# Six 256-column blocks of the second input projection computed in twelve stretches among the mixers' steps

## The reference, cut to what matters

```
a = rms_norm_2(h, norm_attn[i])
u = a @ w_in[i]                                  # 256 x 1024 times 1024 x 3228
(nsa_q, k_cmp, v_cmp, k_slc, v_slc, k_win, v_win, nsa_g,   # 652 columns
 d_q, d_k, d_v,                                  # 3 x 256
 g_q, g_k, g_v, g_lr, g_og,                      # 128, 128, 256, 16, 256
 r_q, r_f, r_i, r_og) = split_cols(u, IN_SPLITS_2)  # 4 x 256
o_a = nsa_attention(...)      # compressed, selected and window attention, gated by sigmoid(nsa_g)
o_b = diff_attention(...)     # two softmax maps per head, subtracted
o_c = gla_mixer(...)          # chunked recurrence, times silu(g_og)
o_d = hgrn2_mixer(...)        # the same recurrence with another gate, times silu(r_og)
h = h + concatenate([o_a, o_b, o_c, o_d]) @ w_out[i]
```

## Time and profile before

| | |
|---|---|
| Runs | 2823.51, 2812.08, 2816.25 us, median 2816.25 |
| Profiled execution | 2825.22 us, of it the span 2823.5 us |
| Busy share | PE 94%, PEld 52%, DVE 22%, ACT 17%, POOL 4% |
| Mean granted clock | 0.922 |

### The profile page before, as it was taken

How to read it: one execution, slowest core, us unless ns; L and a number is a source line. 1 busy time by engine, 2 the same in 40 slices (tenths; PEclk the granted TensorE clock), 3 DMA queues, 4 the chain that set the end, 5 groups by cost and what they waited for, 6 DMA issues and landing times.

```text
span 2823.5 us, 46982 instructions
## 1 busy us (share of the span) xinstructions
PE 2642.1 (94%) x21263; PEld 1474.5 (52%) x21263; DVE 633.8 (22%) x1316; ACT 477.9 (17%) x824; POOL 126.3 (4%) x327
## 2 busy tenths in 40 slices
PE   8899999999989977999999977799999999999997
PEld 7556558666545665444445655444535445353443
DVE  3434523333521432100011432200101000010002
ACT  1421321421222322001012322010000000000001
POOL 4011000011000030000000030000000000000000
PEclk9999999999999756999999756899999999999999
DMA  7321333311334401444434401599999999999990
GB/s 230 115 69 60 119 123 121 130 66 61 120 127 130 133 1 45 134 149 149 143 116 140 131 1 36 211 395 348 368 374 366 385 344 377 369 370 375 355 369 30
DMA packets 181276, 542.26 MB, mean 192 GB/s; under 512 B 26929, under 2 KB 40401, under 8 KB 181073
## 3 DMA queue, kind: packets, MB, share of 16 engines
q1 hardware_dynamic: 167776, 536.95, 52.6%
q10 hardware_dynamic: 12992, 1.22, 0.4%
q0 software_dynamic: 304, 1.05, 0.1%
HBM read 538.12 MB, written 1.05 MB: 191 GB/s over the span
## 4 chain that ended last, share of the span: by engine, by line
PE 89%; ACT 4%; DVE 3%; issue 2%; POOL 1%; DMA 0%; DVEq 0%; SPq 0%; ACTq 0%; POOLq 0%
PE psum L370 27%; PE psum L2310 20%; PE psum L2329 10%; PE psum L529 6%; PE psum L1297 4%; PE psum L2065 3%; PE psum L1958 2%; PE psum L421 1%; PE psum L2285 1%; PE psum L1729 1%; PE psum L2293 1%; PE psum L1708 1%; PE psum L835 1%; PE psum L839 1%; PE psum L2325 1%
## 5 line engine op out<-in xcount | busy, mean ns | idle before, releaser
L370 PE MATMUL psum<-ring,hT 128*128 128x512 f32 (+3 forms) x1856 | 792.5, 586 | 21.6 <-ACT area L642 13.2
L370 PEld LDWEIGHTS psum<-ring,hT 128*128 128x128 f32 x1856 | 355.0, 198 | 417.0 <-issue 384.0
L2310 PE MATMUL psum<-ring,area 128*32 128x448 f32 x4608 | 439.2, 539 | 2.6 <-ACT area L2412 2.0
L2310 PEld LDWEIGHTS psum<-ring,area 128*32 128x32 f32 x4608 | 150.0, 110 | 285.5 <-issue 280.3
L529 PE MATMUL psum<-hT,ring 128*128 128x256 f32 x768 | 170.0, 385 | 0.0
L529 PEld LDWEIGHTS psum<-hT,ring 128*128 128x128 f32 x768 | 148.4, 194 | 21.6 <-issue 1.0
L2329 PE MATMUL psum<-area 128*32 128x256 f32 x2688 | 149.8, 380 | 2.0 <-ACT area L2430 2.0
L2329 PE MATMUL psum<-ring,area 128*32 128x256 f32 x2688 | 151.5, 380 | 0.0
L2310 PE MATMUL psum<-area 128*32 128x448 f32 x1536 | 147.3, 539 | 0.0
L2329 PEld LDWEIGHTS psum<-area 128*32 128x32 f32 x2688 | 85.7, 110 | 60.2 <-ACT area L2430 3.9
L2329 PEld LDWEIGHTS psum<-ring,area 128*32 128x32 f32 x2688 | 84.9, 110 | 57.0 <-issue 2.7
(11 more groups left out here) (491 smaller groups left out, 2462.8 us busy)
## 6 DMA issues: line engine op xcount, KB each, us to landing
ring<-in_w_in_dram SPq DMA_DIRECT2D x92, 1024.0 KB, 5.0
ring<-in_moe_w_gate_dram SPq DMA_DIRECT2D x96, 896.0 KB, 6.8
ring<-in_moe_w_up_dram SPq DMA_DIRECT2D x96, 896.0 KB, 7.7
area<-in_moe_w_down_dram SPq DMA_DIRECT2D x112, 512.0 KB, 7.4
ring<-in_moe_w_down_dram SPq DMA_DIRECT2D x112, 512.0 KB, 6.9
area<-in_moe_w_gate_dram SPq DMA_DIRECT2D x32, 896.0 KB, 6.9
area<-in_moe_w_up_dram SPq DMA_DIRECT2D x32, 896.0 KB, 8.1
ring<-in_w_out_dram SPq DMA_DIRECT2D x16, 1024.0 KB, 5.0
```

Of the source, the lines that this page charges most:

```text
L370: last = nc.tensor.matmul(acc(g)[:, t, 0:d["n"]], lhs(kk, t), w[:, k, :], start=kk == 0, stop=kk == d["nk"] - 1)
L2310: last = nc.tensor.matmul(PS[32 * j:32 * j + 32, 3 * p + b, 0:PIECE], XG[:, k, 32 * b:32 * b + 32], expert_slot(j0 + j // 2, GROUP * (j % ...
```

## The change

The projection's columns are split anew. Four tiles stay in the u stage: 272 columns (g_q, g_k and g_lr), 512 (r_q, r_f), 512 (nsa_q to v_slc) and 396 (k_win, v_win, nsa_g and g_v), 1692 columns. The other 1536 columns are six "fills" of 256 (d_q, d_k, d_v, r_i, g_og, r_og). A fill accumulates both token tiles in one bank, number 2, as 16 matmuls of 256 columns; it yields after every four, and the new plan has its letter f 24 times, always as ff: a stretch is 8 matmuls, half a block, and there are 12. The recurrence gives bank 2 up and goes over two banks, `u % 2`. The norm of d_q and d_k becomes a part of its own (d). The first exponential e stands just after the first g, the two silu gates stand at the end, behind the last fill. The fills' loads stand in LOADS behind those of the compressed attention and ahead of the output projection's. HSB, CS and PCT leave `hT` for the area, as `hT` is read until the last fill.

```diff
-        U_TILES = ((GQ0, GLR0), (GLR0, RQ0), (RQ0, RI0), (NQ0, KW0), (KW0, DK0), (DK0, GQ0), (RI0, COLS2))
+        U_TILES = (((GQ0, GV0), (GLR0, GOG0)), ((RQ0, RI0),), ((NQ0, KW0),), ((KW0, DQ0), (GV0, GLR0)))
+        FILLS = ((DQ0, DK0), (DK0, DV0), (DV0, GQ0), (RI0, ROG0), (GOG0, RQ0), (ROG0, COLS2))
...
+            for piece in FILLS:
+                pieced(("fill", L), A["w_in_2"][L], (piece,), 2)
             pair(("out2", L), A["w_out_2"][L], "dve")
...
         def u_pe(pe, L, fresh):
             gs = group("u", L)
-            for i in range(3):
-                gemm(pe, gs[i], ht_lhs, fresh if i == 0 else None)
-            pe.wait_ge(sem("gemm_out_act"), evacuated(gs[1])[1])
+            gemm(pe, gs[0], ht_lhs, fresh)
+            steps = gemm_steps(pe, [gs[1]], ht_lhs)
+            next(steps)
+            next(steps)
+            pe.wait_ge(sem("gemm_out_act"), evacuated(gs[0])[1])
             transposes(raw((GQ0, P), (GK0, P), (GLR0, 16)), 4).then_inc(sem("m_transposed"), 1)
...
+        def fill_pe(pe, L):
+            for g in group("fill", L):
+                d = TILES[g]
+                gemm_begin(pe, g)
+                landed(pe, d["first"])
+                w = half_view(d["first"], (KD, d["n"]))
+                for t in range(T):
+                    for k in range(KD):
+                        last = nc.tensor.matmul(acc(g)[:, t, :], ht_lhs(k, t), w[:, k, :], start=k == 0, stop=k == KD - 1)
+                        if (t, k) == (T - 1, KD - 1):
+                            last.then_inc(sem("weights_used"), 1)
+                        if k % 4 == 3:
+                            yield
+
+        def fill_act(s, L):
+            for g in group("fill", L):
+                yield
+                yield
+                yield
+                u_out(s, g)
+                yield
...
-        MIXER_PLAN = "cggncvgncgcgtctgacgacegcagcagaaagaeaaagaaagaaagaagaaaggaa"
+        MIXER_PLAN = "cffgencffgcngffcvgffcagcffdcgffdacgacaffadgeaaffgaaagaaffagaaffgaagaagaaffgaagagffv"
...
         def gates_act(s, L):
-            for c in (GOG0, ROG0):
-                s.do(nc.scalar.activation(U2[:, :, c:c + 256], U2[:, :, c:c + 256], ACT.Silu))
             s.after(nc.scalar.activation(GATES.rearrange("p (t g) -> p t g", t=T), U2[:, :, NG0:NG0 + 12], ACT.Sigmoid)
                     .then_inc(sem("m_gates"), 1), "m_gates")
             yield
+            s.do(nc.scalar.activation(U2[:, :, GOG0:GOG0 + 256], U2[:, :, GOG0:GOG0 + 256], ACT.Silu))
+            s.after(nc.scalar.activation(U2[:, :, ROG0:ROG0 + 256], U2[:, :, ROG0:ROG0 + 256], ACT.Silu)
+                    .then_inc(sem("m_gates"), 1), "m_gates")
...
-                if u >= 3:
-                    pe.wait_ge(sem("gla_far"), 16 * L + u - 2)
-                ps = PS[:, u % 3]
+                if u >= 2:
+                    pe.wait_ge(sem("gla_far"), 16 * L + u - 1)
+                ps = PS[:, u % 2]
```

More of the change, by code:

```diff
@@ L253, in pair, with pieced @@
                 TILES.append(dict(group=group, n=512, c0=512 * i, evac=evac, first=first + i, end=first + 3 + i, bank=bank))
-        U_TILES = ((GQ0, GLR0), (GLR0, RQ0), (RQ0, RI0), (NQ0, KW0), (KW0, DK0), (DK0, GQ0), (RI0, COLS2))
+        U_TILES = (((GQ0, GV0), (GLR0, GOG0)), ((RQ0, RI0),), ((NQ0, KW0),), ((KW0, DQ0), (GV0, GLR0)))
+        FILLS = ((DQ0, DK0), (DK0, DV0), (DV0, GQ0), (RI0, ROG0), (GOG0, RQ0), (ROG0, COLS2))
+        def pieced(group, w, pieces, narrow=None):
+            n = sum(b - a for a, b in pieces)
+            per = KD if KD * n <= HALF else KD // 2
+            first = len(LOADS)
+            for k in range(0, KD, per):
+                parts, c = [], 0
+                for a, b in pieces:
+                    parts.append((slice(c, c + b - a), kview(w)[:, k:k + per, a:b]))
+                    c += b - a
+                LOADS.append(((per, n), parts))
+            TILES.append(dict(group=group, n=n, c0=pieces[0][0], pieces=pieces, evac="act", first=first, halves=KD // per,
+                              per=per, nk=KD, end=len(LOADS), narrow=narrow is not None,
+                              bank=2 * (len(TILES) % 2) if narrow is None else narrow))
         CMPW = {}
@@ L1379, in u_pe, with u_out @@
                 .then_inc(sem("gla_z"), 1)
[L1380 to L1383 removed]
+            for _ in steps:
+                pass
+            steps = gemm_steps(pe, [gs[2]], ht_lhs)
+            next(steps)
+            next(steps)
+            pe.wait_ge(sem("gemm_out_act"), evacuated(gs[1])[1])
+            transposes(raw((RQ0, P), (RQ0 + P, P), (RF0, P), (RF0 + P, P)), 6).then_inc(sem("m_transposed"), 1)
+            for _ in steps:
+                pass
+            steps = gemm_steps(pe, [gs[3]], ht_lhs)
+            next(steps)
+            next(steps)
+            pe.wait_ge(sem("gemm_out_act"), evacuated(gs[2])[1])
+            transposes(raw((KC0, P)), 4).then_inc(sem("m_transposed"), 1)
+            for _ in steps:
+                pass
+        def u_out(s, g):
+            d = TILES[g]
+            s.eng.wait_ge(sem("weights_used"), used(d["end"] - 1))
+            c = 0
+            for a, b in d["pieces"]:
+                ins = nc.scalar.activation(U2[:, :, a:b], acc(g)[:, :, c:c + b - a], ACT.Copy)
+                c += b - a
+                if c < d["n"]:
+                    s.do(ins)
+                else:
+                    s.after(ins.then_inc(sem("gemm_out_act"), 1), "gemm_out_act")
         def u_act(s, L):
             gs = group("u", L)
[L1388 to L1395 removed]
+            u_out(s, gs[0])
             s.eng.wait_ge(sem("m_transposed"), 5 * L + 1)
```

152 lines of the change are left out of this document (82 added, 70 removed).

## The result

The changed kernel takes 2794.14 us (median of 4 runs, 2787.21 to 2796.85), the one before on the same chip 2818.46 us (4 runs, 2812.08 to 2823.51): a ratio of 0.991 (95% interval 0.988 to 0.994). It is faster by 24 us, where 57 us were forecast. The time lies in the forecast's wide range, at the weak edge of its mechanism.

What follows compares the result with a forecast made beforehand. PE bounds the u stage; the mixers run at 1.2 GHz with 25.5 us idle. Per layer -41.2 (u stage), +9.5 (mixers), +3 (end): -28.7 us, twice -57: 2768 us profiled, 2758 median; range 2712 to 2818, own range 2738 to 2778.

Steps and rivals of the forecast that it cites:

- The u stage: Second stack's projection stage: three tiles' worth, 48 matmuls of 512 columns, leave; -41.2 us a layer, no new wait.
- The fills: In the mixers: twelve stretches, seven at 3.5 us and five cold at 5.4 us, 52 us a layer; bounds 42.5 to 85.
- The waits: PE's idle time in the mixers: 20 us a layer for 25.5 us; bounds 15 to 35 us.
- The end of the mixers: ACT's copy, table load and two gates behind the last stretch, all on the path: +3 us a layer.
- POOL's wait: PE's 6.7 us wait in the mixers for POOL's factors goes, as the first exponential stands earlier.
- I take it that 5 of 12 start cold: Mixers: five stretches start at the slow clock, a quarter of small work runs slowly; small work 82 us a layer.
- the forecast's scale of 119 to 70 us: PE's work in the mixers other than fills, a layer: 119 us all at slow clock, 70 us all at full clock.
- The first stack: Taken as best analogue for the mixers: small products woven with projection bursts, 40% bursts, mean clock 0.94; fills are 28%.
- Full clock nearly throughout: Rival, mixers: small work 70, fills 42.5, waits 22 us; -48 us a layer, 2720 us; chance 0.18.
- a clock that never rises: Rival, all stretches in the mixers stay slow: 219 us, +36 us a layer, 2889 us; chance 0.06.
- Waits of 35 us: Rival, mixers: ACT's in-order copies make PE wait 35 instead of 20 us a layer; 2788 us; chance 0.14.
- a clock that goes back and forth: Rival, mixers: all twelve stretches start cold, six tenths of small work slow; 182 us, about 2815 us; chance 0.12.

Runs made afterwards that it cites:

- the run with the gates moved: Two silu gates moved ahead of the last attention turn, against the changed kernel with fills respaced and attention exponentials issued early: 2738.33 us, 0.972 of the kernel before.
- fours: Changed kernel with attention exponentials issued early and fills in six stretches of 16 matmuls instead of twelve of 8: 2800.19 us, 0.993 of the kernel before.
- The doubled stretches: Changed kernel with each stretch's 8 matmuls issued twice, the first time without effect: 2854.29 us, 1.015 of the kernel before.
- The second profile of the changed kernel: Changed kernel measured again unaltered, in five rounds: 2792.91 us, 0.991 of the kernel before.
- two banks alone: Kernel before the change with only the recurrence put on two banks instead of three: 2816.78 us, ratio 1.000.
- the first exponential early alone: Kernel before the change with only the plan's first e moved to just behind the first two g: 2804.22 us, ratio 0.995.
- the run with the fills first: Changed kernel with all 24 fill steps at once behind the first compressed step, ahead of the other mixer steps: 2826.53 us, 1.003 of the kernel before.
- the last stretch moved: Changed kernel with the last stretch six steps earlier, right behind the one before it: 2778.75 us, 0.986 of the kernel before.

## Why the prediction was wrong

On the profiled executions the forecast was 2768 us and 2787.2 us came, 19 us more; on the medians the gain was 24 us for 57 us. The difference between the two comparisons is the spread of single executions told above, so the steps are taken from the profiles:

**Right.** The u stage (-41.2 us forecast; -41.2 and -41.2 measured, without a gap). The fills: 52 us forecast, 51.7 and 54.0 measured; 5 and 7 of the 12 stretches took 4.4 us or more, 9 of these 12 less than 5.4 us and one 6.2 us. The waits: 20 us forecast, 20.5 measured. The end of the mixers: +3 forecast, +2.9 measured, and the run with the gates moved shows that it was those 2.5 us of ACT. The two banks: nothing. POOL's wait gone.

**The step that failed: "I take it that 5 of 12 start cold and that a quarter of the small work is done slowly: small work 70 + 0.25 x 49 = 82 us".** Measured were 88.0 and 92.7 us, a share of 0.37 and 0.46; that is 16.7 of the 19 us. The step behind it is the walk through the plan: "The others come after 8 to 14 us". It added up durations at full clock and left out the waits, though the same text counted 20 us of them elsewhere. In the trace six stretches, not four, come after more than 6 us in layer 0 (8.5 to 23.1 us), and the last two after 23.1 and 21.5 us. Both omissions work the same way: the clock falls some 5 us behind a stretch, a wait there uses up some of those fast us, and the rest of the distance runs at the slow clock and is longer still. The last two distances of layer 0 alone hold 28.1 us of small work at the slow clock (15.59 us from 1005 to 1022.85 us, 12.46 us from 1032.3 to 1049.35 us). By the forecast's scale of 119 to 70 us that is an estimated 11.6 us of the 18.0 us above full clock. So the number of cold stretches was nearly right (5 and 7 for 5); what failed is how long the clock stays down before each. The runs show the dependence from both sides: with distances of 16 to 25 us nearly everywhere (fours) the slow share is 0.75 and 0.59, with some 20 short distances 0.14 and 0.08, for the same work.

The first stack is no support for a quarter either, though the mean clock of 0.94 in the earlier trace rows was read rightly: its bursts make up 40%. The doubled stretches make up nearly half of the mixers and still left 0.29 of the small work slow, because the last two distances stayed at 23.1 and 21.5 us. So the share of dense work was the wrong measure to carry over, and distance is a better one.

**What the forecast had not counted: behind the mixers.** The parts of the second stack that stand behind the mixers' closing norms, with unchanged code, took 6.6 us more, counted from the norm's first transpose (391.6 to 394.0 us up to the next layer's u stage, 1089.1 to 1093.2 us to the end). The second profile of the changed kernel has 394.1 and 1093.3 us; of the kernels with the u stage as before, two banks alone has 388.9 and 1088.8 us and the first exponential early alone 393.5 and 1090.8 us. So at least the first 2.4 us are within the spread of unchanged code. A piece of it can be seen where the output projection starts. The windows from 4 us behind the norm's first transpose, before and after:

```profile
1101.00:1105.00 4.00, 4.00 (x8) 1.72 (x7) 0.00 (x0) 0.00 (x0) 0.00 (x0) 0.70 0.00 0
1105.00:1109.00 4.00, 4.00 (x13) 1.80 (x12) 0.00 (x0) 0.00 (x0) 0.00 (x0) 1.00 0.00 0
```

```profile
1071.90:1076.00 4.10, 4.10 (x6) 1.69 (x5) 0.00 (x0) 0.00 (x0) 0.00 (x0) 0.50 0.00 0
1076.00:1080.00 4.00, 4.00 (x10) 1.71 (x9) 0.00 (x0) 0.00 (x0) 0.00 (x0) 0.91 0.01 4
```

The slow start lasted some 2 us longer. It isn't the longer idle time before it: the run with fours has the same 13.1 us of idle and rises as early as the kernel before. Why it differs, and the rest of the 6.6 us, stays open. The first stack's 6.5 us less cancel it by chance: the mixers grew by 38.6 us for 19.0 us, so 19.6 (mixers) - 0.3 (norms) + 6.6 - 6.5 = 19.4 us.

**Its own test.** "The prediction is wrong if the mixers at a mean clock near 0.8 differ from 154 us by more than 12 us, since then the waits were mis-sized." In layer 1 they differ by 13 us at 0.77, and the waits were right all the same. The sentence drew a false line: small work at the slow clock differs by 49 us between the ends, so a mean clock "near 0.8" leaves more than 12 us open.

**The rivals.** Full clock nearly throughout and a clock that never rises are out by the same windows. Waits of 35 us, which would have given 2788 us, name nearly the measured time, but not its reason: they were 20.5 us. The rule of the Trainium skill, "TensorE: Matmul & The Clock Gate", section "A second HAM failure mode: psum-queue depth-cycling", of a clock that goes back and forth bears on part of what happened: 5 and 7 of the 12 stretches began at the slow clock. But re-warming was the smaller part of the price, 9 to 11 us a layer (51.7 and 54.0 us for 43.0 in the run with the fills first); the small work between cost 18 to 23 us (88.0 and 92.7 us for 70).

## What to carry to other kernels

Dense work strewn among small products pays in two ways, by filling waits and by lifting the clock for the others, and the second is lost when the distance between two bursts is long. Count that distance in elapsed time, with waits in it and with the work at the speed that it will have. Here the small work stayed fast for some 5 us behind a burst, whether the burst took 3.7 or 7.2 us, and slow from there to the next one. Place the bursts by the longest distance: 12 bursts of 3.7 us beat 6 twice as long by 48 us (36 of the mixers' 51 us were small work), while going on to 20 or 24 gained 2 to 3 us in the medians, as what the small work won the bursts' slow starts took. Whether a wait that goes pays again as clock is not shown by itself: with the first exponential early alone, layer 0 gained no more than the wait.

## What the runs showed of the hardware

Small products that keep PE busy without a break neither held the clock nor, as a rule, brought it back. It fell with PE busy all the time at 1551 us after and at 948 to 952 us before, and it stayed at 0.50 from 1008 to 1024 us after with PE busy for 4.00 of 4 us in window after window. It can rise on small products, as at 1623 us with the first exponential early alone and once in each layer with the fills first, but that is rare. The Trainium skill, "TensorE: Matmul & The Clock Gate", section "HAM oscillation — how this bites in real kernels", treats the fall as something that idle time of PE brings. The fall at 1005 us, with PE idle, agrees with that; those at 1551 us and at 948 to 952 us don't.

The same program has much the same clock from run to run in one layer, and another in the other layer: small work 88.0 and 88.8 us in layer 0 of the two profiles of the changed kernel, 92.7 and 92.6 us in layer 1, with the same instructions in the same order. Nearly all of this difference is the distance from the eighth to the ninth stretch, over which the clock held in one layer and fell in the other (PE busy for 9.65 and 14.60 us). With the last stretch moved the layers change places, in the small work (93.8 and 88.1 us) and in that distance, 15.8 us in layer 0 and 10.8 us in layer 1. Why the clock falls there in one layer and not in the other stays open. No gain below that size should be put down to a plan from one layer alone.
